# Twelve products of zeros a layer, at three places of the second block's attention stage

## The chip, the cores and the metric

The kernel is one launch on one core of a Trainium2 chip. The metric is the device time of that launch in microseconds, the median of several runs.

## The reference

Two transformer blocks of two layers each work on 256 tokens of 1024 numbers. The change lies in the second block. Each of its layers is a mixing sublayer and then a feed-forward that picks rows of a large table for every token:

```python
def second_block(x, norm1_g, w_in, ...):
    for l in range(DEPTH):                      # DEPTH = 2
        xn = rms_norm_2(x, norm1_g[l])
        x = x + mixing_sublayer(xn, w_in[l], ...)
        xn = rms_norm_2(x, norm2_g[l])
        x = x + peer_ffn(xn, peer_wq[l], peer_keys[l], peer_u[l], peer_v[l])

def mixing_sublayer(xn, ...):
    z = xn @ w_in                               # queries, keys, values, gates of three kinds of heads
    y_sb = stick_breaking_attention(q, k, v)    # weights from a suffix sum of softplus(scores)
    y_ml = mlstm_chunkwise(mq, mk, mv, i, f)    # scores times exp of a decay matrix, with a denominator
    y_sg = spatial_gating(u, v, sg_w, sg_b)
    y = concatenate([y_sb, y_ml, y_sg])
    return y @ w_out

def peer_ffn(xn, wq, sub_keys, u_tab, v_tab):
    q = xn @ wq                                 # 8 heads, two halves of 128
    sv, si = top_k(q . sub_keys, 16)            # then the 16 best of the 16 x 16 sums
    act = x . u_tab[idx]; wgt = gelu(act) * gate
    return sum over 128 picks of wgt * v_tab[idx]
```

The products of zeros have no part in any of this: what they write is never read.

## The kernel before

The program is written by hand for each engine, with semaphores between them; the order on an engine is the order of the calls in its function. The second block's layers are two stages each, `mixing_in` and `mixing_out`. `mixing_in` makes the projections with the weights in two float32r parts, and already starts the attention of the first 128 tokens. `mixing_out`, which the change touches, does the rest of the layer.

The attention heads are in five groups (`groups`, numbers 0 to 4). Groups 0 and 1 hold the queries of the first 128 tokens (t = 0), groups 2, 3 and 4 those of the second 128 (t = 1). Per group TensorE does these pieces: `sb_scores` and `ml_scores` (scores in three partial products, line 1787, in which only 64 rows of the array take part), `ml_rows` (lines 1839 and 1842: a mask with 512 moving columns in bf16, then the decay rows with 6 rows of the array), `suffix_sums` (lines 1852 to 1858), and `sb_values` and `ml_values` (line 1966: weights times values, 64 or 65 moving columns). For a half t it then does `turn_y(t)` (line 1993, eight transposes), `out(t, c)` (line 2009, the output product in two column halves c of eight products), and for the feed-forward `turn_x(t)` (line 2016), `queries(s)` (line 2039) and `key_scores(s)` (line 2050), where step s = 0 and s = 1 are the first two heads of t = 0.

The order on TensorE in `mixing_out` is written out in `pe`, and is what the change edits:

```python
sb_values(0); sb_values(1); ml_values(0); ml_values(1)
sb_scores(pe, 2); ml_rows(pe, 2); ml_rows(pe, 3); turn_y(0)
suffix_sums(pe, 2); suffix_sums(pe, 3); out(0, 0); out(0, 1)
sb_scores(pe, 4); ml_scores(pe, 2); ml_rows(pe, 4); turn_x(0)
ml_values(2); queries(0); suffix_sums(pe, 4); key_scores(0)
sb_values(2); sb_values(3); ml_scores(pe, 4)
ml_values(3); ml_values(4); sb_values(4)
queries(1); key_scores(1); turn_y(1); out(1, 0); out(1, 1)
```

What the others do at these places: ScalarE squares the heads' results (`y_squares`, lines 2110 to 2113), takes roots, and makes exponentials. VectorE sums the squares (`y_sums`, line 2222), scales (`y_scaled`, up to line 2246), copies the transposed half (`take_y`, line 2251), adds `out` to X (line 2258), normalises it (`normed`, line 2269), and from `key_scores` picks the best rows (`first_choice`, `second_choice`, `numbers`, lines 2282 to 2332). When `numbers(0)` is done, GpSimd may issue the gathers (line 1954): 256 a layer, each of 128 rows of the table with 8 KB, so 1 MB. GpSimd holds gathers 2 and later until all values products of the layer are done, gathers 6 and 7 until three of the four `out` halves are done, gather 8 and later until the fourth, and from gather 10 on each waits until the slot that it overwrites was used. After `out(1, 1)` TensorE goes through the 256 rows: VectorE takes a dot product (line 2348), ScalarE the gelu, VectorE builds a diagonal (line 2358) and TensorE adds the row with it (`add_row`, line 2058).

`keep_busy(count)` (lines 188 to 191) issues products of a 128 x 128 block of zeros with 512 columns of zeros in bf16 into PSUM bank 7. Before the change it is called in the first block alone, twice a layer at most with 32 products.

Of the kernel before, what the change touches and what calls it, by code (L numbers as in the profile page):

```python
# [30 lines left out]
P = 128  # L31
# [47 lines left out]
def build(nc, a, out, dbg=None, blocks=(1, 2)):  # L79
    with ExitStack() as ctx:  # L80
# [4 lines left out]
        ZERO = sb("ZERO", [P, 512], BF16)  # L85
# [8 lines left out]
        bank = [ctx.enter_context(nc.psum_tensor(f"bank{i}", [P, 512], F32)) for i in range(8)]  # L94
# [6 lines left out]
        def S(name):  # L101
            if name not in semaphores:
                semaphores[name] = nc.alloc_semaphore(name, row_loaded[-1].num + 1 + len(semaphores))
                numbers_used.add(semaphores[name].num)
            return semaphores[name]
# [7 lines left out]
        def view(ap, *dims, off=0):  # L113

            return bass.AP(ap.tensor, ap.offset + off, [list(ap.ap[0])] + [list(d) for d in dims])
# [3 lines left out]
        def const(name, *dims, parts=P, off=0):  # L119
            for plan, base in ((CONST, None), (CONST1, EXTRA_AT), (CONST2, EXTRA_AT)):  # L120
                if name in plan:
                    at, width = plan[name]
                    ap = CON[0:parts, at:at + width] if base is None else ARENA[0:parts, base + at:base + at + width]
                    return view(ap, *dims, off=off) if dims else ap
# [60 lines left out]
        def stage(**programs):  # L185
            return namedtuple("Stage", programs)(**programs)

        def keep_busy(count):

            for _ in range(count):  # L190
                nc.tensor.matmul(bank[7][:, :], ZERO[:, 0:P], ZERO[:, :], start=True, stop=True)

        def post_norm(turn, done, out_bank, gain, gain_sem, mg, junk):

# [379 lines left out]
        def first_layers():  # L574
# [529 lines left out]
            def feeding(l):  # L1104
# [62 lines left out]
                def pe(pe):  # L1167
                    up_down.pe_early(pe)
                    keep_busy(32)
                    mid.pe(pe)  # L1170
                    up_down.pe(pe)
                    if l + 1 < L:
                        keep_busy(32)
                        pre.pe(pe)
# [63 lines left out]
        def second_layers():  # L1238
# [459 lines left out]
            def mixing_out(l, ring, next_loads):  # L1698
# [32 lines left out]
                def used(x, j):  # L1731
                    t, heads = groups[j]
                    return x[:, 0:(t + 1) * len(heads) * P]
# [55 lines left out]
                def two_scores(to, j, hi, lo, done):  # L1789

                    t, heads = groups[j]
                    for i in range(len(heads)):
                        for kb in range(t + 1):
                            for part in range(3):
                                even = score(to[j], j, i, kb, hi, lo, part)
                                odd = score(to[j + 1], j + 1, i, kb, hi, lo, part)
                    even.then_inc(S(done), 1)
                    odd.then_inc(S(done), 1)

                def last_scores(pe, to, hi, lo, done):  # L1800

                    for i in range(2):
                        for kb in range(2):
                            for part in range(3):
                                last = score(to[4], 4, i, kb, hi, lo, part)
                        if i == 0:
                            last.then_inc(S(done + "_even"), 1)
                            pe.wait_ge(S(done + "_even"), 1)
                    last.then_inc(S(done), 1)

                def sb_scores(pe, j):
                    if j == 0:
                        pe.wait_ge(S("sb_low"), 6)
                    if j == 2:
                        pe.wait_ge(S("sb_arg"), 2)
                    if j == 4:
                        pe.wait_ge(S("sb_arg"), 3)
                        last_scores(pe, sb_bank, sb_hi, sb_lo, "sb_scores")
                    else:
                        two_scores(sb_bank, j, sb_hi, sb_lo, "sb_scores")  # L1820

                def ml_rows(pe, j):

                    t, heads = groups[j]
                    n = len(heads)
                    if j == 0:
                        pe.wait_ge(S("masks_ready"), 1)
                        pe.wait_ge(S("m_ready"), 1)
                    if j == 1:
                        pe.wait_ge(S("cols_taken"), 1)  # L1830
                    if j in (2, 3):
                        pe.wait_ge(S("ml_weight"), 2)
                    if j == 4:
                        pe.wait_ge(S("sb_arg"), 4)
                    if t == 0:
                        masks = view(MASKS[:, 2 * P:3 * P], (0, n), (1, P))
                    else:
                        masks = view(MASKS[:, P:3 * P], (0, n), (1, 2 * P))
                    mm(used(m_bank[j], j), MASKS[:, 0:P], masks, start=True, stop=False, skip_group_check=True)
                    for i, h in enumerate(heads):  # L1840
                        at = i * (t + 1) * P
                        last = mm(m_bank[j][:, at:at + (t + 1) * P], const("pick", (1, P), parts=NH6, off=h * P),
                                  view(m_row[:, t * P:(t + 1) * P], (0, t + 1), (1, P)), start=False, stop=(i == n - 1),
                                  skip_group_check=True)
                    last.then_inc(S("ml_rows"), 1)
# [16 lines left out]
                def ml_scores(pe, j):  # L1862
                    if j == 0:
                        pe.wait_ge(S("ml_low"), 1)
                        pe.wait_ge(S("sg_out"), 1)
                    if j == 2:
                        pe.wait_ge(S("ml_weight"), 4)
                    if j == 4:
                        pe.wait_ge(S("ml_weight"), 5)
                        last_scores(pe, ml_bank, ml_hi, ml_lo, "ml_scores")  # L1870
                    else:
                        two_scores(ml_bank, j, ml_hi, ml_lo, "ml_scores")
# [88 lines left out]
                def pe(pe):  # L1961
                    def values(to, n, j, w, v):
                        t, heads = groups[j]
                        for i, h in enumerate(heads):
                            for kb in range(t + 1):
                                last = mm(to[:, h * n:(h + 1) * n], block(w, j, i, kb), v(kb, h), start=(kb == 0),  # L1966
                                          stop=(kb == t), skip_group_check=True)
                        return last

                    def y_banks_read():  # L1970
                        pe.wait_ge(S("yT_act"), 1)
                        pe.wait_ge(S("yT_dve"), 1)

                    def ml_values(j):
                        if j == 2:
                            y_banks_read()
                        pe.wait_ge(S("ml_probs"), j + 1)
                        values(ML_OUT, 65, j, mlw[j], lambda kb, h: vaug[:, kb, h, :]).then_inc(S("ml_values"), 1)

                    def sb_values(j):  # L1980
                        if j == 0:
                            pe.wait_ge(S("in2_taken_act"), 10)
                            pe.wait_ge(S("in2_taken_dve"), 1)
                        if j == 2:
                            y_banks_read()
                        pe.wait_ge(S("sb_weight"), j + 1)
                        values(SB_OUT, HD, j, lg[j], lambda kb, h: sbv[:, kb, h * HD:(h + 1) * HD]
                               ).then_inc(S("sb_values"), 1)
# [24 lines left out]
                    def turn_x(t):  # L2013
                        pe.wait_ge(S("x_xn"), t + 1)
                        for k in range(KD):
                            last = nc.tensor.transpose(out_banks[t][k // 4][:, k % 4 * P:(k % 4 + 1) * P],
                                                       xn[:, t, k * P:(k + 1) * P], ident)
                            if k % 4 == 3:
                                last.then_inc(S("x_turned"), 1)
# [46 lines left out]
                    ml_values(1)  # L2066
                    sb_scores(pe, 2)
                    ml_rows(pe, 2)
                    ml_rows(pe, 3)
                    turn_y(0)  # L2070
                    suffix_sums(pe, 2)
# [2 lines left out]
                    out(0, 1)  # L2074
                    sb_scores(pe, 4)
                    ml_scores(pe, 2)
                    ml_rows(pe, 4)
                    turn_x(0)
                    ml_values(2)
# [3 lines left out]
                    sb_values(2)  # L2083
                    sb_values(3)
                    ml_scores(pe, 4)
                    ml_values(3)
                    ml_values(4)
                    sb_values(4)
# [510 lines left out]
```

## Time and profile before

| what | value |
| --- | --- |
| runs, us | 2351.45, 2356.65, 2352.45; median 2352.45 |
| the profiled execution, us | 2350.28, with a span of 2348.5 from first to last instruction |
| TensorE busy, share of the span | 88% |
| VectorE busy | 73% |
| ScalarE busy | 35% |
| GpSimd busy | 29% |
| mean granted TensorE clock | 0.955 |
| memory traffic | 700.51 MB, of which the gathers 536.90 MB |

The span is the time between the first and the last instruction of the profiled execution; 1.8 us lie around it. The granted clock is the share of the full 2.4 GHz that TensorE was given; in the trace it is either 1.00 or 0.50 (1.2 GHz) at any moment. The layers of the second block are called the first and the second layer below: `mixing_out` begins at about 788 us in the first and at about 1615 us in the second.

### The profile page before, as it was taken

To read this page: it belongs to the slowest core of one execution; us is meant where nothing else is said; L and a number is where in the kernel's file an instruction comes from. 1 tells how busy PE (TensorE), PEld (TensorE's weight loads), DVE (VectorE), ACT (ScalarE), POOL (GpSimd) and SP (SyncE) were. 2 spreads that over 40 slices of the span, in tenths; PEclk is the share of its full clock that TensorE was granted. 3 is DMA by queue.
4 is the path that set the end of the run, shared out by engine and by line. 5 is a ranking of instruction groups with operands and counts; after the bars stand their busy time and mean duration, and the time that the engine had idled before them with its cause. 6 is when DMAs were issued, how large, how long until landed. Compare 5 with 4: busy or idle time off the path is not lost. (4 is left out here: it accounts for less than half of the span.)

```text
span 2348.5 us, 27740 instructions
## 1 busy us (share of the span) xinstructions
PE 2075.8 (88%) x8629; PEld 1325.4 (56%) x8634; DVE 1717.3 (73%) x4157; ACT 831.4 (35%) x2042; POOL 679.6 (29%) x625
## 2 busy tenths in 40 slices
PE   8999999999979999998788788799999988877787
PEld 6779987679979665544233333297655543322232
DVE  6767777667767477878787777574777787877875
ACT  6656655666647531111111111276312111111110
POOL 2200001200001023444444444110244444444541
PEclk9999999999989889999989999998899999999999
DMA  6354532335535459999999999755499999999996
GB/s 223 117 179 178 185 135 81 143 125 189 184 133 164 179 212 421 417 421 421 421 421 422 421 421 421 297 159 193 177 421 420 421 418 421 421 421 421 421 421 267
DMA packets 138668, 700.51 MB, mean 298 GB/s; under 512 B 14392, under 2 KB 40248, under 8 KB 66872
## 3 DMA queue, kind: packets, MB, share of 16 engines
q0 software_dynamic: 73728, 536.90, 55.2%
q1 hardware_dynamic: 64824, 162.22, 19.8%
q8 instruction: 53, 0.87, 0.2%
q14 instruction: 63, 0.52, 0.1%
HBM read 698.03 MB, written 1.05 MB: 298 GB/s over the span
## 5 line engine op out<-in xcount | busy, mean ns | idle before, releaser
L2058 PE MATMUL bank<-ARENA 128*128 128x512 f32 x2048 | 991.3, 631 | 195.1 <-DVE ARENA L2358 193.9
L2058 PEld LDWEIGHTS bank<-ARENA 128*128 128x128 f32 x2048 | 388.5, 199 | 777.1 <-DVE ARENA L2358 396.9
L1954 POOL DMA_INDIRECT ARENA<-in_uv_rows,ARENA x512 | 581.6, 1136 | 740.9 <-PE bank L2058 626.3
L2348 DVE CUSTOM_DVE_ANT_0 ARENA<-ARENA 128x1024 f32<-128x1024 f32 x512 | 626.0, 1223 | 223.0 <-DMA ARENA<-in_uv_rows,ARENA 215.0
L155 PE MATMUL bank<-PARTS,PARTS 128*128 128x256 f32 (+6 forms) x1488 | 470.1, 316 | 0.0
L154 PE MATMUL bank<-PARTS,PARTS 128*128 128x256 f32 (+3 forms) x1424 | 460.2, 323 | 10.7 <-DVE PARTS L284 6.2
L156 PE MATMUL bank<-PARTS,PARTS 128*128 128x256 f32 (+6 forms) x1488 | 469.5, 316 | 0.0
L2166 ACT ACTIVATE ARENA<-ARENA 128x1 f32<-128x1 f32 x512 | 103.5, 203 | 1009.2 <-DVE ARENA L2348 1008.4
L155 PEld LDWEIGHTS bank<-PARTS,PARTS 128*128 128x128 f32 (+2 forms) x1488 | 284.9, 191 | 13.6 <-issue 1.0
L156 PEld LDWEIGHTS bank<-PARTS,PARTS 128*128 128x128 f32 (+2 forms) x1488 | 284.8, 191 | 13.8
L154 PEld LDWEIGHTS bank<-PARTS,PARTS 128*128 128x128 f32 x1424 | 273.1, 192 | 31.3 <-DVE PARTS L284 7.2
L2358 DVE TENSOR_SCALAR ARENA<-CON,ARENA 128x128 f32<-128x128 f32 x512 | 177.0, 346 | 35.8 <-ACT ARENA L2166 25.7
L537 DVE SCALAR_TENSOR_TENSOR ARENA<-ARENA 128x255 f32<-128x255 f32 x176 | 77.4, 481 | 77.0 <-ACT ARENA L479 70.0
L213 POOL TENSOR_SCALAR STAT<-STAT 128x1 f32<-128x1 f32 x8 | 4.5, 564 | 445.3 <-ACT ARENA L207 445.3
L2039 PE MATMUL bank<-ARENA 128*128 128x128 f32 (+1 forms) x704 | 119.8, 331 | 0.0
L2039 PEld LDWEIGHTS bank<-ARENA 128*128 128x128 f32 x704 | 109.4, 199 | 16.5 <-issue 8.6
L515 DVE TENSOR_TENSOR PARTS<-ARENA,PARTS 128x512 fp32r<-128x512 f32 x176 | 109.5, 686 | 9.1 <-ACT PARTS L457 9.1
L457 ACT CAST PARTS<-ARENA 128x512 fp32r<-128x512 f32 x176 | 95.9, 630 | 10.4 <-PEq L407 10.4
L1360 DVE TENSOR_TENSOR PARTS<-ARENA,PARTS 128x384 fp32r<-128x384 f32 (+2 forms) x160 | 72.3, 485 | 36.4 <-ACT PARTS L1356 36.1
L335 DVE TENSOR_TENSOR PARTS<-ARENA,PARTS 128x512 fp32r<-128x512 f32 (+2 forms) x112 | 68.4, 645 | 29.7 <-ACT PARTS L331 29.2
L1356 ACT CAST PARTS<-ARENA 128x384 fp32r<-128x384 f32 (+2 forms) x160 | 68.8, 460 | 33.3 <-PE bank L156 31.4
L331 ACT CAST PARTS<-ARENA 128x512 fp32r<-128x512 f32 (+2 forms) x112 | 61.7, 580 | 41.7 <-PE bank L156 39.5
(265 smaller groups left out, 1941.2 us busy)
## 6 DMA issues: line engine op xcount, KB each, us to landing
ARENA<-in_w_up_tiles SPq DMA_DIRECT2D x44, 1024.0 KB, 6.4
ARENA<-in_w_down SPq DMA_DIRECT2D x44, 512.0 KB, 3.3
ARENA<-in_w_out SPq DMA_DIRECT2D x32, 512.0 KB, 4.5
ARENA<-in_wq_tiles SPq DMA_DIRECT2D x16, 1024.0 KB, 11.6
ARENA<-in_w_in SPq DMA_DIRECT2D x40, 384.0 KB, 3.9
ARENA<-in_w_in SPq DMA_DIRECT2D x24, 512.0 KB, 9.1
ARENA<-in_w_in SPq DMA_DIRECT2D x40, 256.0 KB, 2.9
ARENA<-in_uv_rows,ARENA POOLq DMA_INDIRECT x512, 21.3
```

Of the source, the lines that this page charges most:

```text
L154: mm(out_ap, w_hi, x_hi, start=start, stop=False, skip_group_check=True)
L155: mm(out_ap, w_lo, x_hi, start=False, stop=False, skip_group_check=True)
L156: return mm(out_ap, w_hi, x_lo, start=False, stop=stop, skip_group_check=True)
L457: nc.scalar.copy(up_hi[s][u], up_raw[s][:, u, :]).then_inc(s_("up_hi"), 1)
L515: nc.vector.tensor_tensor(up_lo[s][u], up_raw[s][:, u, :], up_hi[s][u], ALU.subtract).then_inc(s_("up_lo"), 1)
L537: last = nc.vector.scalar_tensor_tensor(c[:, to], u[:, frm], w, c[:, to], ALU.mult, ALU.add)
L1954: nc.gpsimd.indirect_dma_start(out=slot[slot_of[i]], out_offset=None, in_=table[:, :], in_offset=bass.IndirectOffsetOnAxis(ap=picked[:, t, ...
L2039: last = mm(to, w[:, k, :], x, start=(k == 0), stop=(k == KD - 1), skip_group_check=True)
L2058: last = mm(row_banks[t][n][:, :], diag[i % N_DIAG], slot[slot_of[i]][:, D + n * 512:D + (n + 1) * 512], start=(c == 0), stop=(c == NPICK ...
L2166: nc.scalar.activation(gelu_dots[:, t, c:c + 1], dots[:, t, c:c + 1], ACT.Gelu_apprx_tanh).then_inc(S("gelu_ready"), 1)
L2348: v.tensor_tensor_reduce(u, u, xn[:, t, :], 1.0, 0.0, ALU.mult, ALU.add, dots[:, t, c:c + 1]).then_inc(S("dots_ready"), 1)
L2358: v.tensor_scalar(diag[i % N_DIAG], ident, gelu_dots[:, t, c:c + 1], gate[:, t, c:c + 1], ALU.mult, ALU.mult).then_inc(S("diagonal_ready"), 1)
```

## The change

`keep_busy` takes the bank that it writes as an argument. Four products of zeros are issued at three places in each of the two layers: in `ml_rows(2)`, behind its wait, into bank 7 (called place A below); between `ml_scores(2)` and `ml_rows(4)`, into bank 3 (place B); and between `ml_scores(4)` and `ml_values(3)`, into bank 6 (place C). No wait is added or taken away, and the other engines' programs are as before.

```diff
-        def keep_busy(count):
+        def keep_busy(count, free=7):
 
             for _ in range(count):
-                nc.tensor.matmul(bank[7][:, :], ZERO[:, 0:P], ZERO[:, :], start=True, stop=True)
+                nc.tensor.matmul(bank[free][:, :], ZERO[:, 0:P], ZERO[:, :], start=True, stop=True)
...
                     if j in (2, 3):
                         pe.wait_ge(S("ml_weight"), 2)
+                    if j == 2:
+                        keep_busy(4, 7)
                     if j == 4:
                         pe.wait_ge(S("sb_arg"), 4)
...
                     sb_scores(pe, 4)
                     ml_scores(pe, 2)
+                    keep_busy(4, 3)
                     ml_rows(pe, 4)
                     turn_x(0)
...
                     sb_values(3)
                     ml_scores(pe, 4)
+                    keep_busy(4, 6)
                     ml_values(3)
                     ml_values(4)
```

TensorE at place B before, from the last of the scores on (a row is a line, the operation, what it writes and reads, the moving shape and a count):

```order
L1787 MATMUL bank<-PARTS_1536_5556,PARTS_1536_5555 128x128 x2
L1839 MATMUL bank<-ARENA 128x512
L1842 MATMUL bank<-ARENA 128x256 x2
L2016 MATMUL bank<-CON,ARENA 128x128 x8
L1966 MATMUL bank<-ARENA 128x65 x4
L2039 MATMUL bank<-ARENA 128x128 x16
```

And with the change, where lines behind the edits have numbers higher by 2:

```order
L1787 MATMUL bank<-PARTS_1536_5556,PARTS_1536_5555 128x128 x2
L191 MATMUL bank<-ZERO 128x512 x4
L1841 MATMUL bank<-ARENA 128x512
L1844 MATMUL bank<-ARENA 128x256 x2
L2018 MATMUL bank<-CON,ARENA 128x128 x8
L1968 MATMUL bank<-ARENA 128x65 x4
L2041 MATMUL bank<-ARENA 128x128 x16
```

Four products stand ahead of `ml_rows(4)`, and nothing else has moved.

## Rows read from the trace of the kernel before

**Rows 1.** Page: the span.

```profile
span 2348.5 us, 27740 instructions
```

**Rows 2.** Stretches: length, busy us of PE, PEld, DVE, ACT, POOL, granted clock, DMA share, GB/s.

```profile
900.00:1480.00 580.00, 495.25 (x1218) 223.91 (x1218) 451.98 (x1182) 92.62 (x300) 262.75 (x230) 0.94 1.01 421
1720.00:2320.00 600.00, 502.88 (x1252) 225.06 (x1252) 465.92 (x1213) 94.33 (x309) 269.55 (x236) 0.96 1.01 421
1688.00:1692.00 4.00, 4.00 (x11) 1.85 (x10) 3.77 (x10) 0.41 (x2) 2.38 (x2) 1.00 0.60 184
```

**Rows 3.** Timeline of POOL: gather 8 of each layer (start, us, what, idle before).

```profile
868.07 0.94 POOL L1954 DMA_INDIRECT ARENA<-in_uv_rows,ARENA  x1 [4.28 <-PE bank L2009]
...
1695.69 0.94 POOL L1954 DMA_INDIRECT ARENA<-in_uv_rows,ARENA  x1 [4.18 <-PE bank L2009]
```

**Rows 4.** Timeline of PE, first layer.

```profile
798.24 1.97 PE L1993 MATMUL bank<-CON,ARENA 128*128 128x128 f32 x8 [2.23 <-DVE ARENA L2246]
801.63 1.22 PE L1856 MATMUL bank<-ARENA,CON 128*128 128x256 f32 x2 [1.43 <-DVE ARENA L1755]
...
806.91 14.01 PE L2009 MATMUL bank<-ARENA 128*128 128x512 f32 x32
...
824.28 2.07 PE L1842 MATMUL bank<-ARENA 6*128 6x256 f32 x4
826.28 1.97 PE L2016 MATMUL bank<-CON,ARENA 128*128 128x128 f32 x8
...
833.94 0.60 PE L1856 MATMUL bank<-ARENA,CON 128*128 128x256 f32 x2
...
835.23 0.61 PE L2050 MATMUL bank<-ARENA 128*128 128x128 f32 x4
...
843.20 6.13 PE L2039 MATMUL bank<-ARENA 128*128 128x128 f32 x32
...
851.89 1.10 PE L1993 MATMUL bank<-CON,ARENA 128*128 128x128 f32 x8 [1.37 <-DVE ARENA L2246]
853.83 13.97 PE L2009 MATMUL bank<-ARENA 128*128 128x512 f32 x32 [0.84 <-issue]
```

**Rows 5.** Timeline of PE, second layer.

```profile
1626.56 1.97 PE L1993 MATMUL bank<-CON,ARENA 128*128 128x128 f32 x8
...
1629.80 1.22 PE L1856 MATMUL bank<-ARENA,CON 128*128 128x256 f32 x2 [1.27 <-DVE ARENA L1755]
...
1634.14 13.90 PE L2009 MATMUL bank<-ARENA 128*128 128x512 f32 x32
...
1652.70 1.09 PE L2016 MATMUL bank<-CON,ARENA 128*128 128x128 f32 x8 [0.20 <-DVE ARENA L2269]
...
1659.57 0.61 PE L2050 MATMUL bank<-ARENA 128*128 128x128 f32 x4
...
1668.54 4.83 PE L2039 MATMUL bank<-ARENA 128*128 128x128 f32 x32
...
1676.64 1.16 PE L1993 MATMUL bank<-CON,ARENA 128*128 128x128 f32 x8 [1.60 <-DVE ARENA L2246]
1678.57 16.85 PE L2009 MATMUL bank<-ARENA 128*128 128x512 f32 x32 [0.78 <-issue]
```

**Rows 6.** Stretches: the clock around places A and B (columns as in rows 2).

```profile
794.00:806.00 12.00, 8.34 (x23) 6.20 (x23) 6.91 (x19) 10.94 (x23) 0.00 (x0) 0.50 1.02 410
825.00:830.00 5.00, 5.00 (x22) 4.25 (x21) 3.03 (x5) 4.34 (x7) 0.00 (x0) 0.50 0.00 0
1617.00:1632.00 15.00, 13.73 (x56) 10.18 (x56) 8.04 (x23) 9.95 (x18) 0.00 (x0) 0.50 0.97 383
```

**Rows 7.** The zeros of the first block, L191, from 130 to 160 us.

```profile
L191 PEld LDWEIGHTS bank<-ZERO x32: 95/97/101, 136.5 to 143.0; 128*128 128x128 bf16 x32
```

**Rows 8.** Timeline of ACT and DVE, second layer: end of the squares, start of their sum.

```profile
1668.78 0.49 ACT L2113 ACTIVATE ARENA<-bank 128x384 f32<-128x384 f32 x1 [0.91 <-PE bank L1966]
...
1671.02 1.21 DVE L2222 TENSOR_REDUCE STAT<-ARENA 128x16 f32<-128x1024 f32 x1
```

## The prediction

> **What bounds the kernel now.** I read the page first, then the stretches, then the timelines of the engines around the three places. The span is 2348.5 us [rows 1]. In both layers the long stretch in which table rows are streamed keeps the DMA engines at a share of 1.01 and 421 GB/s, while TensorE is busy for 495 of 580 us in the one and 503 of 600 in the other [rows 2]. There the transfers set the time, and TensorE's clock (0.94 and 0.96) costs nothing. So an edit ahead of that stretch counts only by how much earlier or later the stream gets going, and that shift then passes to the end of the layer one for one.
>
> What holds the stream's start? Gather 8 is issued when `out(1, 1)` ends: GpSimd sat idle 4.28 and 4.18 us before it, released by line 2009 [rows 3]. In the second layer the queue has run dry before that (share 0.60 and 184 GB/s from 1688 to 1692 us, at a time when TensorE is still in `out`) [rows 2]. So the end of `out(1, 1)` is the point to watch in each layer. Followed back from there (by start and length in [rows 4] and [rows 5]), the path has three pieces:
>
> - Piece 1, TensorE: from `suffix_sums(2)` to the end of `key_scores(0)`. First layer 801.63 to 835.84, 34.2 us; second layer 1629.80 to 1660.18, 30.4 us.
> - Piece 2, ScalarE and VectorE: the choice of the rows of the first head, then `y_sums(1)` and `y_scaled(1)`. It ends where `turn_y(1)` starts, released by VectorE's line 2246 after TensorE idled 1.37 and 1.60 us. 16.05 and 16.46 us. What TensorE does meanwhile is beside the path.
> - Piece 3, TensorE: `turn_y(1)` and `out(1, ·)`. 851.89 to 867.80, 15.9 us; 1676.64 to 1695.42, 18.8 us.
>
> The start of piece 1 is set by VectorE (idle 1.43 and 1.27 us ahead of line 1856, until its line 1755).
>
> The same work is longer at the low clock. Granted clock was 0.50 from 794 to 806, from 825 to 830 and from 1617 to 1632 us [rows 6]. The 32 records of `out` took 13.97 us when the clock was high and 16.85 us when they began low; eight transposes 1.1 or 1.97 us [rows 4, 5]. The falls do not come at the same place of the program in both layers: the one during `ml_rows(4)` is in the first layer alone, that ahead of `out(1, ·)` in the second alone. I take from this that each has a chance of coming or not in any one run.
>
> **The cost of one product.** The 32 products of zeros of the first block start 136.5 to 143.0 us [rows 7]: 6.5 us over 31 steps, 0.21 us each at the high clock. Four are 0.84 us. At 1.2 GHz I take double, 1.68 us, since six products of line 1856 to 1858 took 5.28 us low in the first layer (801.63 to 806.91) and three of them 1.29 us high (833.94 to 835.23) [rows 4], which is a factor of 2.05.
>
> **Place A**, in front of `ml_rows(2)`. In the first layer TensorE idles 2.23 us before `turn_y(0)`, which covers 0.84 us and even 1.68 us; without that cover it would be paid in full only if the 1.43 us ahead of the suffix sums were gone too. Cost 0. In the second layer the clock is low by then and `turn_y(0)` started without an idle. It would end 1.68 us later, at 1628.53 + 1.68 = 1630.21, which is 0.41 us after the suffix sums started: +0.4 us. What A could give is a high clock in the suffix sums, all of them 2.58 us instead of 5.28 and 4.34 us, so up to -2.7 and -1.8 us. But behind A come `ml_rows`, with 6 of 128 rows of the array, and then idle time, the same sort of work that preceded the present falls, and I expect most of the restored clock to be lost again. I take -0.9 for both layers together beside the +0.4, near the small end, so **-0.5 us** for A, between -4.5 and +0.4.
>
> **Place B**, in front of `ml_rows(4)`. It lies in piece 1, on TensorE, with almost no cover: `turn_x(0)` waited 0.20 us for VectorE in the second layer [rows 5]. At the high clock it costs 0.84 - 0.20 = 0.64 us a layer. Behind it in the queue stand `ml_rows(4)`, `turn_x(0)`, `queries(0)` and `key_scores(0)`, and VectorE waits for the last. What it can give is seen by the two layers against each other. From the end of `out(0, ·)` to the end of `key_scores(0)` the first took 835.84 - 820.92 = 14.9 us with the fall in it, the second 1660.18 - 1648.04 = 12.1 us without: 2.8 us. If B prevents the fall in the first layer it gives 2.8 - 0.6 = -2.2 us there, and +0.6 in the second: **-1.6 us**. Bounds: no fall prevented and the four products run low, +1.7 in the first and +0.6 in the second, +2.3; or falls prevented in both layers of a run that had both, -4.3.
>
> **Place C**, in front of `ml_values(3)`. It is in the time of piece 2. Its products push `ml_values(3)`, `ml_values(4)`, `sb_values(4)` and so ScalarE's squares, but the squares were done at 1669.27 and their sum began only at 1671.02, when VectorE had finished `numbers(0)` [rows 8]: 1.75 us of cover, and even the low-clock price of 1.68 fits. The gathers from number 2 on wait for the same values products, which end before the first gather starts. `queries(1)` took 6.13 and 4.83 us with the low clock [rows 4, 5] and would be shorter, but TensorE then only waits longer for VectorE. So C gives nothing directly. What it touches is piece 3: the more TensorE idles ahead of `turn_y(1)`, the likelier `out(1, ·)` begins at the low clock. That is 16.85 - 13.97 = 2.9 us a layer, one layer of the two has it now. I take a third of it as the added risk, **+1.0 us**, between -2.9 (the second layer gets rid of it) and +2.9 (the first gets it too).
>
> A rule of the Trainium skill bears on this place. The row: the eight transposes at 851.89 ran in 1.10 us, and `out` behind them ran high throughout [rows 4]. The page "TensorE: Matmul & The Clock Gate", section "Part 4: PE-mode transpose", says that a transpose in transpose mode does not count as activity for the clock. By that rule `turn_y(1)` would do nothing to hold the clock, `out(1, ·)` would start low in both layers whenever `queries(1)` ends early, and C would be worth +2.9 instead of +1.0, for a sum of +0.8. The first layer's row neither proves nor excludes it, since `queries(1)` ended late there.
>
> **The sum.** -0.5 - 1.6 + 1.0 = -1.1 us. Against the profiled execution's own 2350.28 that is 2349.2; it is 2.2 us below the median of the runs, so against the median I predict 2352.45 - 1.1 = **2351.4 us**. The three runs spread over 5.2 us, which fits falls of the clock that come or do not come.
>
> **Rivals.**
> 1. *The clock stays high from the suffix sums to the end of `out(1, ·)` in both layers.* That gives -2.7 and -1.8 (suffix sums), -2.2 and +0.6 (B), and -2.9 (second layer's `out(1, ·)`): -9.0 us, 2343.5. For it: each single fall has a layer without it, except the low suffix sums. Against it: both layers enter the suffix sums low, and nothing is added in the long waits for VectorE that precede them and `out(1, ·)`. Chance 0.12.
> 2. *The cover moves and `out(1, ·)` starts low in the first layer too (the slower one).* Place: piece 3. With the clock high through `queries(1)`, that would end earlier than at 843.20 + 6.13 = 849.3: at the high clock its 6.13 us shrink to at least 6.13 / 2.05 = 3.0, so it ends near 847, and TensorE waits some 5 us instead of 2.6 (851.89 - 849.3, less `key_scores(1)`) before `turn_y(1)`, and the fall comes before `out(1, ·)`: +2.9. With B costing 0.6 in both layers and A 0.4, and no fall prevented that would have come, this is 2.9 + 1.2 + 0.4 = +4.5; with B's four products low in one layer +5.4: 2357.9. It decides from the point where the idle ahead of `turn_y(1)` is long enough for a fall and B saved none. The same page's section "Why this matters for your kernels" says that an idle gap between bursts returns the clock to half. Chance 0.12.
> 3. *Zeros do nothing for the clock, so the change doesn't do what it says.* Then only the prices are left: A 0.4, B 1.7 and 0.6, C 0: +2.7, 2355.2. Against it: behind the zeros of the first block the clock was high, but dense work follows them there. Chance 0.14.
> 4. *All of it is hidden by the transfers*, which would finish the first eight gathers no earlier anyway: 0, 2352.4. Against it: the dry 4 us of the second layer [rows 2]. Chance 0.08.
>
> **How the numbers follow.** The forecast has 0.54. What can be told from no change in this kernel is about 0.2%, 4.7 us. The forecast and rivals 3 and 4 lie within it, save for the tails of the forecast: A and B both at their good ends reach -8, but each layer would have to get every chance. Of rival 1 0.09 is over the limit, with 0.02 from the forecast: faster 0.11. Of rival 2 some 0.07, and 0.01 from the forecast: slower 0.08. The same: 0.81. The range that leaves out no more than 2 in 10 is 2346.4 to 2356.4: below, the forecast with one more prevented fall in each layer (-5), above, rival 3 with the spread of the runs.
>
> **What would show it.** In the changed profile: four records of line 191 at each place, steps 0.21 us or double; the clock at 1.00 through `ml_rows(4)` and `turn_x(0)` (four records of line 1844 in 1.1 us, not 2.07), and 12.7 us instead of 14.9 from `out(0, ·)` to `key_scores(0)`; the sum of squares still right behind `numbers(0)`; and a longer idle before `turn_y(1)`. If `out(1, ·)` takes some 17 us in both layers, rival 2 is right. If the clock falls between B and `turn_x(0)` all the same, rival 3. The prediction is wrong if the time moves by over 5 us, or if the stream's start no longer follows the end of `out(1, 1)`.

## The result, and the profile after

The changed kernel is slower. Over 20 runs its median is 2362.24 us (2352.14 to 2367.99); the kernel before, in 20 runs of its own, has 2354.86 us (2348.94 to 2360.10). The ratio is 1.0025, with a 95% interval of 1.0016 to 1.0034, which is +5.9 us (+3.8 to +8.0); the two medians alone differ by 7.4 us. What a kernel's times gave is told below in the same way, as its ratio less 1, times 2355 us. 2351.4 us had been forecast, with a range up to 2356.4.

The profiled execution took 2362.15 us:

```profile
span 2360.4 us, 27782 instructions
```

Against [rows 1] that is 11.9 us more, but the profile of before was one of its fastest runs, and not all of the difference lies in the stage: 2.3 us had passed before `mixing_out` of the first layer began. From the first record of `sb_values(0)` to the issue of gather 8, which I call the **lead** below, the first layer took 84.0 us instead of 80.3, the second 82.0 instead of 81.0. That is 4.6 us of the 11.9. The last 5.0 us lie outside the stage too, 2.5 in the two streams, 1.3 between the layers and 1.2 behind the last row. The streams run at the rate they had (stretches of the changed kernel; columns as in [rows 2]):

```profile
910.00:1490.00 580.00, 488.37 (x1221) 221.00 (x1219) 450.44 (x1179) 92.52 (x300) 256.66 (x230) 0.96 1.01 421
1730.00:2330.00 600.00, 504.32 (x1251) 226.63 (x1252) 465.50 (x1212) 94.31 (x308) 274.75 (x236) 0.96 1.01 421
1696.00:1704.00 8.00, 8.00 (x20) 3.53 (x19) 7.62 (x18) 0.92 (x5) 2.06 (x2) 1.00 0.79 292
```

421 GB/s again, and from 1696 to 1704 us, while TensorE is still in `out`, the queue again runs short (share 0.79, 292 GB/s). Gather 8 still waits for `out(1, 1)`, as in [rows 3] (timeline of POOL, changed kernel):

```profile
874.01 1.91 POOL L1956 DMA_INDIRECT ARENA<-in_uv_rows,ARENA  x1 [4.58 <-PE bank L2011]
...
1705.61 0.94 POOL L1956 DMA_INDIRECT ARENA<-in_uv_rows,ARENA  x1 [4.50 <-PE bank L2011]
```

TensorE in the first layer of the changed kernel, timeline, to be held against [rows 4] (line numbers are higher by 2; of four products of zeros the trace sometimes lacks a record):

```profile
796.88 1.13 PE L1844 MATMUL bank<-ARENA 6*128 6x256 f32 x4
800.51 1.97 PE L1995 MATMUL bank<-CON,ARENA 128*128 128x128 f32 x8 [2.50 <-DVE ARENA L2250]
803.90 1.22 PE L1858 MATMUL bank<-ARENA,CON 128*128 128x256 f32 x2 [1.42 <-DVE ARENA L1755]
...
809.18 13.97 PE L2011 MATMUL bank<-ARENA 128*128 128x512 f32 x32
...
826.41 1.49 PE L191 MATMUL bank<-ZERO 128*128 128x512 bf16 x3 [0.17 <-issue]
...
828.25 2.07 PE L1844 MATMUL bank<-ARENA 6*128 6x256 f32 x4
830.26 1.97 PE L2018 MATMUL bank<-CON,ARENA 128*128 128x128 f32 x8
...
833.62 5.22 PE L2041 MATMUL bank<-ARENA 128*128 128x128 f32 x32
...
839.98 0.61 PE L2052 MATMUL bank<-ARENA 128*128 128x128 f32 x4
...
844.24 0.81 PE L191 MATMUL bank<-ZERO 128*128 128x512 bf16 x3 [0.16 <-issue]
...
847.51 3.79 PE L2041 MATMUL bank<-ARENA 128*128 128x128 f32 x32
...
856.64 1.97 PE L1995 MATMUL bank<-CON,ARENA 128*128 128x128 f32 x8 [1.23 <-DVE ARENA L2250]
859.03 14.71 PE L2011 MATMUL bank<-ARENA 128*128 128x512 f32 x32 [0.42 <-issue]
```

Three things stand there. The suffix sums start 1.42 us behind an idle and run low, as before: A kept the clock high through `ml_rows(3)`, but changed nothing on the path. The products of place B run at the low clock (three records in 1.49 us, where those of place C take 0.81), `ml_rows(4)` and `turn_x(0)` take 2.07 and 1.97 us as before, and `queries(0)` has become longer, 5.22 us. From the end of `out(0, ·)` at 823.15 to the end of `key_scores(0)` at 840.59 pass 17.4 us instead of 14.9. And `queries(1)`, behind C, does run at the high clock now (3.79 us instead of 6.13), but then the transposes and the start of `out(1, ·)` are low. The clock in stretches of the first layer (changed kernel):

```profile
827.00:836.00 9.00, 9.00 (x35) 7.06 (x33) 3.26 (x5) 4.98 (x9) 0.00 (x0) 0.50 0.00 0
838.00:853.00 15.00, 13.08 (x105) 12.23 (x104) 11.31 (x42) 4.05 (x8) 1.23 (x1) 1.00 0.01 1
854.00:860.00 6.00, 4.14 (x13) 3.00 (x14) 3.71 (x12) 3.21 (x9) 3.75 (x4) 0.50 0.95 351
```

The second layer (timeline of PE, against [rows 5]) had no fall at place B and pays B's high price, 12.7 us instead of 12.1; there the products of place C run low:

```profile
1660.26 0.81 PE L191 MATMUL bank<-ZERO 128*128 128x512 bf16 x3 [0.16 <-issue]
...
1669.14 0.61 PE L2052 MATMUL bank<-ARENA 128*128 128x128 f32 x4
...
1673.77 1.48 PE L191 MATMUL bank<-ZERO 128*128 128x512 bf16 x3 [0.33 <-issue]
...
1686.35 1.04 PE L1995 MATMUL bank<-CON,ARENA 128*128 128x128 f32 x8
1689.67 15.67 PE L2011 MATMUL bank<-ARENA 128*128 128x512 f32 x32 [2.28 <-issue]
```

In this layer C reached the path by a way that I had not looked at. `turn_y(1)` started without an idle, right behind `key_scores(1)`, and `out(1, ·)` 3.3 us behind the start of `turn_y(1)`, where before it was 1.9. The first of its products needs the part of the transposed half that ScalarE copies (`take_y`), and on ScalarE that copy stands behind the one of `key_scores(1)` and a table load. With `key_scores(1)` late, ScalarE was late too (timeline of ACT; the last line is from before):

```profile
1686.55 0.37 ACT L2158 COPY ARENA<-bank 128x256 f32<-128x256 f32 x1 [0.82 <-PE bank L2052]
1686.94 1.28 ACT L2165 ACT_TABLE_LOAD   x1
...
1688.45 1.12 ACT L2130 ACTIVATE ARENA<-bank,GAINS 128x128 f32<-128x128 f32 x4
...
1677.33 1.14 ACT L2126 ACTIVATE ARENA<-bank,GAINS 128x128 f32<-128x128 f32 x4 [0.27 <-PE bank L1993]
```

Before, ScalarE waited 0.27 us for the transposes, which had started at 1676.64; in the changed kernel they had started at 1686.35, and it came to them 2.1 us later without a wait.

### The profile page after: what moved, and what is told of

It is laid out like the page before. It is cut to its first block and busy times, and to the rows that moved or that the text cites. A ratio compares the mean times of both kernels' runs of the same rounds, so it can differ in the third digit from the quotient of the medians.

```text
span 2360.4 us, 27782 instructions
## 1 busy us (share of the span) xinstructions
PE 2075.6 (88%) x8647; PEld 1327.5 (56%) x8658; DVE 1717.8 (73%) x4157; ACT 830.9 (35%) x2042; POOL 680.1 (29%) x625
## 6 DMA issues: line engine op xcount, KB each, us to landing
ARENA<-in_wq_tiles SPq DMA_DIRECT2D x16, 1024.0 KB, 12.1
```

## The experiments

Three theories were on the table. **Price:** the products are paid where TensorE has no wait, and the clock falls all the same. **Out starts low:** C empties the time ahead of `turn_y(1)` (rival 2 of the prediction). **Moved fall**, which became **tied fall:** where the clock falls is tied to the work ahead of it, and the zeros act or fail by where they stand to that point.

### One place at a time

Each is the changed kernel without the other two places:

```diff
 a_only:   -keep_busy(4, 3)   -keep_busy(4, 6)
 b_only:   -keep_busy(4, 7)   -keep_busy(4, 6)
 c_only:   -keep_busy(4, 7)   -keep_busy(4, 3)
```

> Place A alone, four products of zeros in front of ml_rows(2). Theory 'price' (each product is paid where TensorE has no wait in front of it, and the clock falls all the same): 0 in the first layer, +0.4 us in the second where they run low, so +0.4 us against the kernel before. Theory 'moved fall' (the zeros shift where in the program the clock falls, and a place not looked at pays): anything from -4 to +4 us, with the suffix sums or out(0) longer or shorter than 5.28 and 13.9 us. Theory 'out starts low' (C drains the work ahead of turn_y(1)): no effect of A.

> Place B alone, four products in front of ml_rows(4). Theory 'price': +0.6 us a layer at the high clock, +1.7 us at the low, so +1.3 to +3.4 us. Theory 'moved fall': the fall during ml_rows(4) is prevented or not; prevented it gives -1.6 us, and a fall that begins with the products costs up to +3.4 us in that layer, since the low time also ends later. Theory 'out starts low': +1.3 us at most.

> Place C alone, four products in front of ml_values(3). Theory 'price': 0, it lies beside VectorE's choice of rows (1.75 us of cover). Theory 'out starts low': +2 to +6 us, with out(1) at 15 to 17 us in both layers and TensorE idle for some 5 us before turn_y(1). Theory 'moved fall': between -3 and +3 us.

Measured: A alone 1.0001 (0.9992 to 1.0010), B alone 1.0018 (1.0007 to 1.0030), C alone 1.0006 (0.9995 to 1.0017). In us +0.2, +4.2 and +1.4, together 5.8, which is what the whole change costs (5.9). So B is most of it, and its +4.2 lies above the upper bound that the prediction had given it, +2.3, though its interval (+1.6 to +7.1) reaches below that. It is also above what theory "price" allowed (+3.4). Where it comes from, the second layer of B alone shows (timeline of PE):

```profile
1654.22 1.79 PE L191 MATMUL bank<-ZERO 128*128 128x512 bf16 x4
...
1656.36 2.07 PE L1842 MATMUL bank<-ARENA 6*128 6x256 f32 x4
1658.37 1.97 PE L2016 MATMUL bank<-CON,ARENA 128*128 128x128 f32 x8
...
1661.73 5.16 PE L2039 MATMUL bank<-ARENA 128*128 128x128 f32 x32
```

It is the changed kernel's first layer over again: the fall at the very start of the zeros, all four low (1.79 us), and everything up to `queries(0)` low, 17.4 us in all. The first layer of the same run had no fall and took 12.7 us. C alone (timeline of PE, first layer and then the second) has rival 2's shape:

```profile
841.92 3.79 PE L2039 MATMUL bank<-ARENA 128*128 128x128 f32 x32
...
850.97 1.97 PE L1993 MATMUL bank<-CON,ARENA 128*128 128x128 f32 x8 [1.62 <-DVE ARENA L2247]
853.36 15.24 PE L2009 MATMUL bank<-ARENA 128*128 128x512 f32 x32 [0.42 <-issue]
...
1682.85 1.97 PE L1993 MATMUL bank<-CON,ARENA 128*128 128x128 f32 x8 [1.61 <-DVE ARENA L2247]
1685.24 15.73 PE L2009 MATMUL bank<-ARENA 128*128 128x512 f32 x32 [0.42 <-issue]
```

The clock is held through values and `queries(1)`, which end 5.3 us before `turn_y(1)` instead of 2.6; it is low when VectorE lets TensorE go on, and `turn_y(1)` and `out(1, ·)` take 17.6 us here and 18.1 in the second layer. The interval of C alone takes in no change, so C's share is likely but not proven by the times.

What the two do to this last piece is seen only when layers of one kind are compared. In layers whose suffix sums take 5.28 us, `turn_y(1)` and `out(1, ·)` took 15.9 us wherever B and C were absent (six of six in the profiles of before, of A alone and of the products in the waits below), 18.1 with C alone, 18.6 with B alone and 17.1 with both (with B one step earlier, below, 17.4 and 15.9). In layers with shorter suffix sums they were already long before, 18.8 and 17.4 us. So B costs time there too, behind the place where it stands: in B's second layer the clock fell again just as `turn_y(1)` began.

### The same products with 6 rows of the array

```diff
-                nc.tensor.matmul(bank[free][:, :], ZERO[:, 0:P], ZERO[:, :], start=True, stop=True)
+                nc.tensor.matmul(bank[free][:, :], ZERO[0:NH6, 0:P], ZERO[0:NH6, :], start=True, stop=True)
```

(for the twelve products of the second block alone, in a function of its own, `keep_few`; the products of the first block stay as they are.)

> All three places, the twelve products as long as before (512 columns) but with 6 of the 128 rows of the array. If the zeros act through the clock, rows should matter, and this kernel differs from the changed one: theory 'price' (no help from the zeros) has it equal to the changed kernel within 1 us, so about +6 us against the kernel before; theory 'moved fall' has it 2 us or more away from the changed kernel, upward if the full zeros do prevent some falls; theory 'out starts low' has it faster than the changed kernel by 2 to 4 us, since the clock then falls earlier and queries(1) ends later.

Measured: 1.0022 (1.0011 to 1.0034), +5.2 us, equal to the changed kernel, as "price" had it and "moved fall" had not. For the change as it stands, the full zeros gain nothing on balance over zeros that hardly touch the array. Taken alone this would speak for "price"; the last experiment shows that rows do matter, and that these three places are the wrong ones. The trace shows it even here, at place A (timeline of PE, 6 rows, first layer, against 796.88 above):

```profile
796.29 1.03 PE L196 MATMUL bank<-ZERO 6*128 6x512 bf16 x4
...
800.20 2.07 PE L1849 MATMUL bank<-ARENA 6*128 6x256 f32 x4
```

In layers with suffix sums of 5.25 to 5.28 us the clock fell 5.4 to 6.0 us behind the first record of `sb_values(0)` without A, 5.4 us with A at 6 rows, and 8.9 to 9.5 us with A at 128 rows (four layers). It gains nothing, since the path waits for VectorE there.

### The kernel before, a second profile

No edit.

> The kernel before, unchanged, for a second profile. Theory 'tied fall': each layer again shows one of the two patterns seen so far: values at the high clock, suffix sums 5.28 us, and 14.9 us from the end of out(0) to the end of key_scores(0); or values at the low clock, suffix sums 4.3 us, and 12.2 us. Theory 'free fall' (the fall comes anywhere): lengths in between.

One execution, 2354.49 us. The first layer now showed the pattern that the second had in [rows 5] and the second that of [rows 4]: suffix sums 4.44 and 5.28 us, and from the end of `out(0, ·)` to the end of `key_scores(0)` 12.1 and 14.9 us. "Tied fall" had expected just these two patterns, "free fall" lengths in between (second layer, timeline of PE):

```profile
1654.17 2.07 PE L1842 MATMUL bank<-ARENA 6*128 6x256 f32 x4
```

Over the profiles of before, of the change, of A, B and C alone, of the 6-row products and of the filler kernel below there are 16 layers. In the ten whose suffix sums took 5.25 to 5.28 us the clock fell 3.1 to 3.4 us behind the end of `out(0, ·)`; of the six with shorter ones, five had no fall there and one had it at 4.8 us. The scores end 3.0 to 3.1 us behind `out(0, ·)`. So the fall, where it comes, comes just when B's products begin.

The traces also show that the fall keeps its distance from the rise before it. In all ten layers the clock rose within 0.6 us of the start of `out(0, ·)` and fell 17.1 us after that rise. `out(0, ·)` itself takes 13.9 to 14.2, which leaves the 3.1 to 3.4 us. Why the distance is this one no run shows. In the five layers without the fall the clock rose 0.8 to 1.0 us before `out(0, ·)` began, which is why part of their suffix sums ran high, and stayed high for 30 us or more. In the kernel before, first layer (stretches):

```profile
807.20:824.10 16.90, 16.84 (x69) 8.64 (x68) 2.90 (x6) 2.67 (x6) 0.43 (x1) 1.00 0.00 1
824.30:831.00 6.70, 6.70 (x27) 5.86 (x27) 3.73 (x5) 5.46 (x9) 0.00 (x0) 0.50 0.00 0
```

### B one step earlier

```diff
                     sb_scores(pe, 4)
+                    keep_busy(4, 3)
                     ml_scores(pe, 2)
```

without A, B and C; and the changed kernel with B moved in this way, A and C kept.

> Four products of zeros a layer as at place B, but one step earlier, between sb_scores(4) and ml_scores(2), so ahead of the point 3.3 to 3.4 us behind the end of out(0) at which the clock fell in all four layers that had this fall with or without B. Theory 'tied fall' (the point of the fall is tied to the work by the rise before it; B's products start just when it has happened, run low and lengthen the low time): here the fall goes away, 14.9 us from the end of out(0) to the end of key_scores(0) become 12.7, and layers without the fall pay 0.6; together -3 to +1 us against the kernel before, 4 to 7 us faster than B alone. Theory 'price' (zeros hold nothing anywhere): +1.3 to +4 us, like B alone (+4.3).

> The changed kernel with one thing moved: B's four products stand between sb_scores(4) and ml_scores(2), one step earlier, and A and C are as in the change. Theory 'tied fall': from the end of out(0) to the end of key_scores(0) it takes 13.0 us in every layer (17.4 or 12.7 in the changed kernel), and the kernel is 2 to 6 us faster than the changed one, so 0 to +4 us against the kernel before, the rest being C's. Theory 'price': no difference from the changed kernel, +6 us.

Measured: B early alone 0.9999 (0.9987 to 1.0012), the changed kernel with B early 1.0006 (0.9995 to 1.0017), both in the range of "tied fall". In the first layer of B early alone (timeline of PE, and a stretch), whose suffix sums took 5.28 us and whose clock rose 0.3 us behind the start of `out(0, ·)`, there is no fall:

```profile
827.30 1.04 PE L191 MATMUL bank<-ZERO 128*128 128x512 bf16 x4
...
830.07 1.13 PE L1842 MATMUL bank<-ARENA 6*128 6x256 f32 x4
...
833.06 3.81 PE L2039 MATMUL bank<-ARENA 128*128 128x128 f32 x32
```

```profile
811.90:842.50 30.60, 30.48 (x167) 20.45 (x167) 10.41 (x30) 11.03 (x20) 0.55 (x1) 1.00 0.00 1
```

All four layers of the two kernels took 13.0 us for the part, 0.3 more than expected for B early alone. Three of the four had suffix sums of 5.26 to 5.28 us, the kind of layer in which the clock had fallen ten times out of ten. The products now begin 1.7 us behind the end of `out(0, ·)` instead of 3.0: a step of 1.3 us decides between +4.2 us and nothing that can be told from no change. B early gives about as much as it costs: 13.0 us against a mean of 13.5 in the four layers of before (14.9, 12.1, 12.1, 14.9).

### Products in the waits only

```diff
                     key_scores(1)
+                    keep_busy(6, 6)
                     turn_y(1)
+                    keep_busy(3, 6)
                     out(1, 0)
```

> No products at A, B and C. Six between key_scores(1) and turn_y(1), where TensorE idles 1.4 to 3 us for VectorE, and three between turn_y(1) and out(1, 0). Theory 'tied fall' and theory 'out starts low' alike: the clock holds, turn_y(1) takes 1.1 us and out(1) 13.9 to 14.0 us in both layers instead of up to 16.9, which is 0 to -3 us a layer, about -2 us in all. Theory 'price': 0 to +1 us, out(1) as before.

Measured: 0.9990 (0.9975 to 1.0005), -2.4 us, not clear of no change. In both layers `turn_y(1)` and `out(1, ·)` together took 15.9 us, against 15.9, 18.8, 17.4 and 15.9 in the four layers of before, a mean of 17.0. That would be 1.1 us a layer and fits the time. But both layers of this profile had suffix sums of 5.28 us, and in such layers the piece took 15.9 us without any products too. So this profile doesn't show that they did anything; neither does the time. The next two kernels say more: with products here as well, all their four layers took 15.9 us.

### Every thin stretch, and the version that wins

```diff
 sb_values(0)'s wait;       +keep_busy(3, 2)
 ml_rows(2)'s wait;         +keep_busy(4, 7)
 ml_rows(pe, 3)             +keep_busy(4, 1)
 turn_y(0)                  +keep_busy(8, 1)        trimmed: (5, 1)
 sb_scores(pe, 4)           +keep_busy(4, 3)        trimmed: (2, 3)
 key_scores(1)              +keep_busy(6, 6)
 turn_y(1)                  +keep_busy(3, 6)
```

(each behind the call or wait that it is named with, none at B or C.)

> Products of zeros in every thin stretch: three in front of sb_values(0), four at A, four behind ml_rows(3), eight behind turn_y(0), four between sb_scores(4) and ml_scores(2), six and three around turn_y(1). Theory 'tied fall': if the clock stays high from values to out(1), the suffix sums take 2.6 us instead of 4.3 to 5.3, less 0.6 to 1.3 us of price on the path: -3 to -8 us in all; where it has fallen before all the same, the products run low and it costs +3 to +6 us a layer. Theory 'price': +8 us or more.

> The kernel with products in every thin stretch, trimmed where they overran: five instead of eight behind turn_y(0), where the suffix sums started 1.7 us late, and two instead of four between sb_scores(4) and ml_scores(2), which cost 0.85 us. Theory 'tied fall': up to 2 us a layer less than with eight and four, so -4 to -8 us against the kernel before; if two and five are too few to hold or restore the clock, suffix sums take 4 to 5 us again and it is -1 to -3 us. Theory 'price': still +4 us or more.

Measured: 0.9988 (0.9974 to 1.0002), -2.8 us, not clear of no change and just short of the -3 to -8 expected, and, trimmed, **0.9975 (0.9964 to 0.9986)**: -5.9 us (-8.5 to -3.3), median 2349.87 against 2353.95 (the medians alone differ by 4.1). This beats the kernel before and the changed one. The first layer of the trimmed kernel (timeline of PE) and stretches of the first layer and the second:

```profile
799.51 1.24 PE L191 MATMUL bank<-ZERO 128*128 128x512 bf16 x5
801.99 0.70 PE L1858 MATMUL bank<-ARENA,CON 128*128 128x256 f32 x2 [1.23 <-DVE ARENA L1755]
...
804.68 13.90 PE L2012 MATMUL bank<-ARENA 128*128 128x512 f32 x32
...
849.11 13.97 PE L2012 MATMUL bank<-ARENA 128*128 128x512 f32 x32 [0.19 <-issue]
```

```profile
788.00:834.00 46.00, 43.12 (x250) 29.55 (x249) 18.84 (x52) 24.18 (x48) 0.55 (x1) 1.00 0.39 149
1618.50:1625.20 6.70, 6.03 (x18) 3.31 (x19) 3.77 (x10) 6.55 (x12) 0.00 (x0) 0.50 0.95 386
```

In the first layer the clock is at 1.00 from the first values product to `key_scores(0)`. In the second it still fell, at 1618.4, and was back at 1625.2, in time for the suffix sums. So these products do not hold the clock everywhere, but where it fell all the same it was high again before `out(0, ·)`. Suffix sums take 2.7 and 2.8 us instead of 5.28 and some 4.4 (801.99 to 804.68 in the first layer), the part behind `out(0, ·)` 12.6, `out(1, ·)` 13.97, and the leads are 75.2 and 76.1 us. In both layers of the untrimmed kernel the clock fell ahead of `turn_y(0)`, the eight zeros behind it ran low and pushed the suffix sums 1.6 to 1.8 us out; that is what trimming took away.

### The trimmed kernel with 6 rows

```diff
-keep_busy(n, b)
+keep_few(n, b)
```

at all seven places of the trimmed kernel, where `keep_few` uses 6 rows of `ZERO` as above.

> The trimmed kernel with products in every thin stretch, each with 6 of the 128 rows of the array instead of all, of the same length and at the same places. Theory 'tied fall' with rows that count: the products cost what they cost but hold no clock, so suffix sums take 4.3 to 5.3 us again, and 15 to 17 us pass from the end of out(0) to the end of key_scores(0): +3 to +9 us against the kernel before, 8 us or more above the trimmed kernel. Theory 'order alone' (the trimmed kernel gains by its order, not by the clock): equal to the trimmed kernel.

Measured: 1.0077 (1.0061 to 1.0093), +18 us; the same products at the same places with all rows gave -5.9. Even against "tied fall", which had +3 to +9, that is twice as much. Its first layer (a stretch and the timeline of PE):

```profile
791.00:814.00 23.00, 23.00 (x82) 14.96 (x82) 8.82 (x24) 12.34 (x26) 0.00 (x0) 0.50 0.74 291
```

```profile
807.84 2.31 PE L196 MATMUL bank<-ZERO 6*128 6x512 bf16 x5
```

TensorE was busy for all of those 23 us, at half the clock. Suffix sums took 5.0 and 5.3 us, and the fall behind `out(0, ·)` came at 2.9 and 3.4 us, with two of these products at the place of B early. Nearly half of the time lost lies ahead of the suffix sums: the products, twice as long at the low clock, pushed them to 20 us behind the first record of `sb_values(0)` instead of 14 or 15. The gain of the trimmed kernel is the clock's, then, and whether such products hold it depends on the rows of the array that they use, not on their keeping the engine busy. Only 6 and 128 rows were tried.

### The leads, side by side

Lead of the first and second layer in each profile, in us; twice the difference of their mean from that of before (80.3, over four layers); and what the times gave:

| kernel | leads | from the leads | from the times |
| --- | --- | --- | --- |
| before, two profiles | 80.3, 81.0; 79.1, 80.7 | | |
| changed | 84.0, 82.0 | +5.4 | +5.9 |
| A alone | 80.2, 80.9 | +0.6 | +0.2 |
| B alone | 79.5, 85.8 | +4.8 | +4.2 |
| C alone | 79.4, 82.9 | +1.7 | +1.4 |
| 6 rows | 83.3, 82.7 | +5.4 | +5.2 |
| B early | 79.9, 78.6 | -2.0 | -0.2 |
| changed, B early | 80.4, 80.0 | -0.2 | +1.4 |
| products in the waits | 80.5, 83.1 | +3.1 | -2.4 |
| every thin stretch | 77.3, 77.5 | -4.5 | -2.8 |
| trimmed | 75.2, 76.1 | -8.0 | -5.9 |
| trimmed, 6 rows | 94.0, 88.8 | +24 | +18 |

(For the last three, whose lead begins behind three products, 0.63 us a layer is added.) Outside the kernel with products in the waits, whose second layer began with the clock low already (values products in 5.35 us instead of 2.86 or 4.1), one profile's leads come within about 2 us of the times, and within 6 in the last row. That the time passes from the lead to the end one for one holds: from gather 8 to the last add of the layer every profile had 646 to 648 us.

By pieces, against the mean of before's two profiles and for both layers together, the changed kernel's +5.4 us are +3.1 from the end of `out(0, ·)` to the end of `key_scores(0)`, +2.1 in `turn_y(1)` and `out(1, ·)`, and +0.2 elsewhere. B alone has +3.1, +1.8 and -0.2, C alone 0.0, +1.8 and -0.1.

## Why the prediction was wrong

- **What bounds it** was right. The stream runs at the same 421 GB/s, gather 8 waits for `out(1, 1)`, and the table above finds the time in the lead.
- **The step that failed is B's gain**, "If B prevents the fall in the first layer it gives 2.8 - 0.6 = -2.2 us there", booked as -1.6 us; measured +4.2. It rested on the premise under the three pieces, "each has a chance of coming or not in any one run", and on taking it, without a row that showed it, that four products in front of `ml_rows(4)` would come in time. The falls are not free: in the pattern with slow suffix sums the clock falls 3.1 to 3.4 us behind `out(0, ·)`, and B's products start at that moment. [Rows 4] had the fact, had I taken the difference of two of its rows: `out(0, ·)` ends at 820.92, and `ml_rows(4)` is low from its start at 824.28. Products behind the fall cannot prevent it. And the bound was too small: I counted four low products, +1.7, but not that the low time itself gets longer. It was 6.8 us in before and 10.2 us in both layers of this pattern with B at full rows, so `queries(0)` pays too: 17.4 - 14.9 = +2.5 us in such a layer, +0.6 in one without the fall, +3.1 together. What B did to `turn_y(1)` and `out(1, ·)`, +1.8 us in the profile of B alone, the prediction had at nothing.
- **C's** +1.0 us was of the right size as far as can be told (+1.4, interval -1.2 to +4.0), in C alone by the mechanism given: off the path itself, its price is a longer idle and a low start of `turn_y(1)` and `out(1, ·)`, 17.9 us on average instead of 17.0. "So C gives nothing directly" did not hold in the second layer of the changed kernel, where C's products ran low. The squares became a bound, by little (ScalarE and VectorE, against [rows 8]): they ended at 1680.79, and their sum began at 1680.82, some 0.2 us later behind `numbers(0)` than before, so the 1.75 us of cover were used up and a little more. And ScalarE, held up by the late `key_scores(1)`, started `out(1, ·)` 1.4 us later, as shown above.

```profile
1680.30 0.49 ACT L2117 ACTIVATE ARENA<-bank 128x384 f32<-128x384 f32 x1 [0.91 <-PE bank L1968]
...
1680.82 1.22 DVE L2226 TENSOR_REDUCE STAT<-ARENA 128x16 f32<-128x1024 f32 x1
```

- **A's** -0.5 us against +0.2 (-1.9 to +2.4). In three of the four layers of the changed kernel and of A alone it held the clock longer, through `ml_rows(2)` and `ml_rows(3)` (1.13 us where the low row has 2.07), and lost it again in the wait before the suffix sums, as expected. The gain looked for there is real, but takes products in all the waits up to the suffix sums.
- **Rival 2**, the slower one, came nearest, with +4.5 to +5.4 (by the prediction's own prices the latter is 4.5 - 0.6 + 1.7 = +5.6). It was right in sign and in where the cover goes: `queries(1)` ended 5.3 us before `turn_y(1)` in the first layer, and `out(1, ·)` started low. But it had 2.9 us for that piece and at most 2.3 for B, where the changed kernel's leads have 2.1 and 3.1, and the loss was not C's alone.
- **Rival 3**, that zeros do nothing for the clock, gave 2355.2. By the prediction's own sign for it, a fall between B and `turn_x(0)`, it looked right for this change, and the 6-row products cost the same; but it falls by the last experiment, -5.9 against +18 us.
- **Rival 1** did not come: the clock fell in both layers of the changed kernel. **Rival 4**, that the transfers hide it all, falls by the 646 to 648 us behind gather 8, whatever the lead.
- **The rule on transposes** in the Trainium skill, "TensorE: Matmul & The Clock Gate", section "Part 4: PE-mode transpose", would have put the sum at +0.8, nearer than mine. No run here isolates it: where `out(1, ·)` began high, products or `queries(1)` stood close ahead of the transposes.
- The time before was known from three runs, 2352.45; over 20 it is 2354.86. With the -1.1 that makes 2353.8, still 8.5 us below the measured median.

What stays open is why a layer falls into the one pattern or the other, how B's products lead to a low start of `out(1, ·)` some 30 us later, whether B one step earlier would fail with 6 rows when nothing else is changed, and whether other counts of products in the seven waits do better than the first trimming.

## What to carry to other kernels

Before dense filler is put near a fall of TensorE's clock, take the fall's time against the last long dense piece ahead of it, in several layers or runs: it may be tied to the work, and filler can prevent it only from ahead; behind it, it runs low and costs double. Filler belongs into waits of TensorE that something else sets, in counts that fit the wait at the clock that it will run at. And an edit that makes TensorE finish early ahead of a wait can pay for it with a low clock after the wait.

## What the runs showed of the hardware

- The falls of the clock repeat at the same place of the program. Ten layers of seven kernels with a suffix-sum time of 5.25 to 5.28 us had theirs 3.1 to 3.4 us behind the end of the same product and 17.1 us behind the rise before it, though absolute times differ by up to 4.6 us in the first layer and 7.5 in the second.
- Whether products hold the clock depends on the rows they use. With 6 of 128 rows in the added products, TensorE was busy for 23.0 of 23 us at a granted clock of 0.50; with all rows, the same order of instructions had 1.00 over 46 us in the first layer, and fell for under 7 us in the second.
- Products of zeros can help to hold the clock at 1.00: the products added in that kernel held nothing but zeros.
- With B's four products the low time around them was 10.2 us instead of 6.8, so 1.8 us of low products made the part longer by 2.5 us.
